# One record of 512 columns for the high weights times high and low activations, in the products that VectorE adds to the residual

## What is computed

```python
# first block
u = causal_dwconv(h @ w_up[l], ffn_conv_w[l], ffn_conv_b[l])
u_gate, u_val = jnp.split(u, 2, axis=-1)
x = x + gate_f * ((jax.nn.silu(u_gate) * u_val) @ w_down[l])
...
# second block, per layer
h = h + hybrid_mixer(rmsnorm(h, norm_mix_g[layer]), ...)       # ends in y @ w_mix_out
h = h + memory_cross_attention(rmsnorm(h, norm_x_g[layer]), ...)   # ends in o @ w_xo
hn = rmsnorm(h, norm_ffn_g[layer])
h = h + swiglu(hn, ffn_w_gate[i], ffn_w_up[i], ffn_w_down[i])   # layer 0
```

## Time and profile before

| | |
|---|---|
| median of 3 runs | 2247.67 us (2243.6 to 2249.77) |
| profiled execution | 2247.01 us, span 2245.3 us |
| TensorE busy | 2183.2 us (97%) |
| VectorE busy | 1701.4 us (76%) |
| ScalarE busy | 1296.6 us (58%) |
| DMA | 563.82 MB, mean 251 GB/s |
| mean granted TensorE clock | 0.99 of 2.4 GHz |

### The profile page before, as it was taken

The page is one execution under the profiler, slowest core; times in us unless marked ns, Lnnn a source line. Parts: engine busy times, 40 slices in busy tenths (PEclk is TensorE's granted clock), DMA queues, the critical chain, the costliest instruction groups (busy, mean ns, idle before and its releaser), DMA issues.

```text
span 2245.3 us, 34129 instructions
## 1 busy us (share of the span) xinstructions
PE 2183.2 (97%) x13631; PEld 1948.4 (87%) x13631; DVE 1701.4 (76%) x1889; ACT 1296.6 (58%) x1289; POOL 76.1 (3%) x159
## 2 busy tenths in 40 slices
PE   7999999999999999999999999999999999999997
PEld 5989988999989899999898888888887888888886
DVE  6768967884785465558654888888888888888887
ACT  3564434763425444443344777777777777777775
POOL 5002200000000000000000000000000000000000
PEclk9999999999999999999999999999999999999999
DMA  9746858655635366555372799999999999999995
GB/s 287 193 127 217 269 175 236 175 173 178 175 116 173 104 170 177 181 155 156 116 239 81 268 365 361 369 329 365 359 369 350 321 370 362 364 345 358 365 365 184
DMA packets 414601, 563.82 MB, mean 251 GB/s; under 512 B 17098, under 2 KB 268212, under 8 KB 414448
## 3 DMA queue, kind: packets, MB, share of 16 engines
q1 hardware_dynamic: 409680, 555.26, 73.5%
q0 software_dynamic: 4768, 6.36, 1.2%
HBM read 559.75 MB, written 1.84 MB: 250 GB/s over the span
## 4 chain that ended last, share of the span: by engine, by line
PE 83%; DVE 8%; ACT 2%; issue 1%; DVEq 0%; ACTq 0%
PE pair L1174 59%; PE misc L1174 13%; PE pair L1234 4%; DVE wlo L1808 2%; DVE opf L1876 2%; PE misc L1717 1%; DVE wlo L2157 1%; PE pair L1685 1%; ACT whi L674 1%; PE misc L1274 1%; PE misc L1253 0%; DVE hl L1827 0%; PE misc L1694 0%; PE misc L1695 0%; PE misc L1365 0%
## 5 line engine op out<-in xcount | busy, mean ns | idle before, releaser
L2157 DVE TENSOR_TENSOR wlo<-raw,whi 128x2048 fp32r<-128x2048 f32 x336 | 764.2, 2290 | 119.6 <-ACT whi L1056 118.9
L1056 ACT CAST whi<-raw 128x2048 fp32r<-128x2048 f32 x336 | 643.1, 1917 | 205.0 <-PE pair L1174 123.5
L1808 DVE TENSOR_TENSOR wlo<-raw,whi 128x2048 fp32r<-128x2048 f32 (+2 forms) x158 | 348.5, 2209 | 157.9 <-ACT whi L674 157.2
L1174 PE MATMUL pair<-hh,whi 128*128 128x256 f32 x1408 | 405.5, 288 | 8.4 <-DVE opl L1827 4.1
L1174 PE MATMUL pair<-hl,whi 128*128 128x256 f32 x1408 | 400.7, 285 | 0.0
L1174 PE MATMUL pair<-hh,wlo 128*128 128x256 f32 x1408 | 400.4, 284 | 0.0
L1174 PE MATMUL pair<-whi,oph 128*128 128x512 f32 x896 | 353.5, 395 | 5.2 <-issue 4.5
L1174 PE MATMUL pair<-wlo,oph 128*128 128x512 f32 x896 | 350.0, 391 | 0.0
L1174 PE MATMUL pair<-whi,opl 128*128 128x512 f32 x896 | 349.7, 390 | 0.0
L674 ACT CAST whi<-raw 128x2048 fp32r<-128x2048 f32 (+2 forms) x158 | 290.1, 1837 | 84.7 <-PE pair L1174 66.8
L1174 PE MATMUL pair<-oph,whi 128*128 128x256 f32 x976 | 279.4, 286 | 5.2 <-issue 3.0
(11 more groups left out here) (464 smaller groups left out, 2788.1 us busy)
## 6 DMA issues: line engine op xcount, KB each, us to landing
raw<-in_moe_w_gate_dram SPq DMA_DIRECT2D x112, 1024.0 KB, 7.1
raw<-in_moe_w_up_dram SPq DMA_DIRECT2D x112, 1024.0 KB, 7.3
raw<-in_moe_w_down_dram SPq DMA_DIRECT2D x112, 1024.0 KB, 7.0
raw<-in_w_in_dram SPq DMA_DIRECT2D x38, 1024.0 KB, 6.1
raw<-in_w_mod_dram SPq DMA_DIRECT2D x24, 1024.0 KB, 5.7
raw<-in_w_up_dram SPq DMA_DIRECT2D x44, 512.0 KB, 5.2
raw<-in_w_xkv_dram SPq DMA_DIRECT2D x16, 1024.0 KB, 5.7
raw<-in_ffn_w_gate_dram SPq DMA_DIRECT2D x22, 512.0 KB, 4.1
```

Source lines behind the costliest of these rows:

```text
L1056: act.copy(whi[:, q, :], raw[:, r, :]).then_inc(sem("hi_ready"), 1)
L1174: ins = pe.matmul(out_, lhs, rhs, start=start and i == 0, stop=stop and i == 2)
L1808: dve.tensor_tensor(wlo[:, i_ % SPLIT, 0:size], raw[:, raw_of(n), 0:size], whi[:, i_ % SPLIT, 0:size].bitcast(F32), ALU.subtract).then_inc ...
L2157: dve.tensor_tensor(wlo[:, q, :], raw[:, r, :], whi[:, q, :].bitcast(F32), ALU.subtract).then_inc(sem("lo_ready"), 1)
```

## The change

High and low activations are laid out as one tensor each: `hx` holds `hh` and `hl`, `opx` holds `oph` and `opl`, so that one operand can reach both parts of a chunk. Five stages stand in `TWO_SUMS`. In these, a triple becomes two matmuls (`both`): the high weights times both parts of the activations, in one record of 512 columns whose operand is two stretches of 256 with a jump between them, into the two halves of a bank; then the low weights times the high activations, 256 columns, into the first half. The bank then holds two sums: the second half has the high weights times the low activations, and VectorE adds it to the residual too, before the first half, each addition waiting for the one before (`link`). `up2` has code for the same form, but is not in the list, and so keeps `three`, as do all other stages.

```diff
+TWO_SUMS = ("down", "mixout0", "mixout1", "xo0", "down2")
...
-        hh = sb("hh", [P, DC, T], F32R)
-        hl = sb("hl", [P, DC, T], F32R)
+        hx = sb("hx", [P, 2, DC, T], F32R)
+        hh, hl = hx[:, 0], hx[:, 1]
...
-        oph = sb("oph", [P, 24, T], F32R)
-        opl = sb("opl", [P, 24, T], F32R)
+        opx = sb("opx", [P, 2, 24, T], F32R)
+        oph, opl = opx[:, 0], opx[:, 1]
...
+            def both(out_, w_hi, w_lo, x, start, stop):
+
+                pe.matmul(out_.rearrange("p (k t) -> p k t", k=2), w_hi, x, start=start, stop=False)
+                return pe.matmul(out_[:, 0:T], w_lo, x[:, 0], start=False, stop=stop)
...
                             col = slice(m * P, (m + 1) * P)
-                            ins = three(pair[:, q, m, 0:T], wh[:, col], wl[:, col], operand(xh, x), operand(xl, x), start, stop)
+                            parts = operand(x_parts, x)
+                            if groups[g][0] in TWO_SUMS:
+                                ins = both(pair[:, q, m, :], wh[:, col], wl[:, col], parts, start, stop)
+                            else:
+                                ins = three(pair[:, q, m, 0:T], wh[:, col], wl[:, col], parts[:, 0], parts[:, 1], start, stop)
...
+            def second(g):
+
+                return pair[:, pair_seq[g] % PAIRS, :, T:2 * T]
+
             def add_modulated(g, j, gate):
                 ps = group(g)
+                if groups[g][0] in TWO_SUMS:
+                    for m in range(2):
+                        t = 2 * j + m
+                        ins = dve.scalar_tensor_tensor(xT[:, t], second(g)[:, m], mod[:, gate + t:gate + t + 1], xT[:, t], ALU.mult, ALU.add)
+                    link(ins)
...
             def add_plain(g, j):
                 ps = group(g)
+                if groups[g][0] in TWO_SUMS:
+                    link(dve.tensor_tensor(xT[:, 2 * j:2 * j + 2, :], second(g), xT[:, 2 * j:2 * j + 2, :], ALU.add))
                 dve.tensor_tensor(xT[:, 2 * j:2 * j + 2, :], ps, xT[:, 2 * j:2 * j + 2, :], ALU.add).then_inc(sem("dve_read"), 1)
...
                     for j, g in enumerate(stage_groups["down2"]):
                         ps = group(g)
-                        link(dve.tensor_tensor(down_n, ps, rt[:].unsqueeze(1).to_broadcast([P, 2, T]), ALU.mult))
+                        by_token = rt[:].unsqueeze(1).to_broadcast([P, 2, T])
+                        link(dve.tensor_tensor(down_n, second(g), by_token, ALU.mult))
+                        link(dve.tensor_tensor(xT[:, 2 * j:2 * j + 2, :], down_n, xT[:, 2 * j:2 * j + 2, :], ALU.add))
+                        link(dve.tensor_tensor(down_n, ps, by_token, ALU.mult))
                         dve.tensor_tensor(xT[:, 2 * j:2 * j + 2, :], down_n, xT[:, 2 * j:2 * j + 2, :], ALU.add)\
                             .then_inc(sem("dve_read"), 1)
```

More of the change, by code:

```diff
@@ L1276, in sums, with into_norm @@
                     ins.then_inc(sem("squares_summed"), 1)
-            def into_norm(stage, name, xh, xl, beside=None, **how):
+            def into_norm(stage, name, x_parts, beside=None, **how):
                 each = how.pop("each_chunk", None)
                 for j, g in enumerate(stage_groups[stage]):
-                    dense_group(g, xh, xl, each_chunk=each if j == 0 else None, **how)
+                    dense_group(g, x_parts, each_chunk=each if j == 0 else None, **how)
                     if j >= 1:
@@ L1475, in _ @@
             for i, g in enumerate(stage_groups["up"]):
-                dense_group(g, hh, hl, each_chunk=h_chunk(1) if i == 0 else None)
+                dense_group(g, hx, each_chunk=h_chunk(1) if i == 0 else None)
                 if i == 0:
@@ L1483, in _ @@
             pe.wait_ge(sem("mem_ready"), DC)
-            into_norm("down", "mix0", oph, opl, beside=stage_groups["xk0"][0], each_chunk=lambda c: (sem("u_lo"), c + 1))
+            into_norm("down", "mix0", opx, beside=stage_groups["xk0"][0], each_chunk=lambda c: (sem("u_lo"), c + 1))
             for l in range(2):
@@ L1491, in _ @@
                     for g in stage_groups[f"{stage}{l}"]:
-                        dense_group(g, hh, hl, each_chunk=h_chunk(k0) if first else None)
+                        dense_group(g, hx, each_chunk=h_chunk(k0) if first else None)
                         first = False
@@ L1609, in _ @@
                 if l == 0:
-                    into_norm("xo0", "ffn0", hh, hl, each_chunk=lambda c: (sem("xo_lo"), c // 2 + 1))
+                    into_norm("xo0", "ffn0", hx, each_chunk=lambda c: (sem("xo_lo"), c // 2 + 1))
                     for i, g in enumerate(stage_groups["up2"]):
-                        dense_group(g, *fin, each_chunk=h_chunk(NORM["ffn0"]) if i == 0 else None)
+                        dense_group(g, fin_at, each_chunk=h_chunk(NORM["ffn0"]) if i == 0 else None)
                         if i == 0:
@@ L1618, in _ @@
                     pe.wait_ge(sem("mem_ready"), 2 * DC)
-                    into_norm("down2", "mix1", lambda c: up2_out(0, c), lambda c: up2_out(1, c), beside=stage_groups["xk1"][0],
+                    into_norm("down2", "mix1", up2_parts, beside=stage_groups["xk1"][0],
                               each_chunk=lambda c: (sem("u2_lo"), c + 1))
@@ L1641, in _ @@
             for j, g in enumerate(stage_groups["xo1"]):
-                dense_group(g, hh, hl, each_chunk=(lambda c: (sem("xo_lo"), 4 + c // 2 + 1)) if j == 0 else None)
+                dense_group(g, hx, each_chunk=(lambda c: (sem("xo_lo"), 4 + c // 2 + 1)) if j == 0 else None)
                 if j >= 1:
@@ L2331, in _ @@
                                 dve.wait_ge(sem("up2_silu"), j - 2)
-                            dve.tensor_tensor(gate_n[:, j % 3], ps[:, 0], rt[:], ALU.mult).then_inc(sem("up2_gate"), 1)
+                            if groups[ups2[j]][0] in TWO_SUMS:
+                                dve.wait_ge(sem("up2_second"), j + 1)
+                                both = up_sum[:, j % 3]
+                                link(dve.tensor_tensor(both, ps, both, ALU.add))
+                            else:
+                                both = ps
+                            dve.tensor_tensor(gate_n[:, j % 3], both[:, 0], rt[:], ALU.mult).then_inc(sem("up2_gate"), 1)
                         if j >= 1:
```

45 lines of the change are left out of this document (26 added, 19 removed).

## The result

| | before | changed |
|---|---|---|
| median of 19 runs | 2248.28 us (2243.6 to 2251.98) | 2254.95 us (2248.34 to 2262.71) |
| ratio, 95% interval | | 1.0029 (1.0019 to 1.0039) |
| profiled execution | 2247.01 us, span 2245.3 | 2249.94 us, span 2248.2 |
| mean granted clock over the runs | 0.989 | 0.987 |

The changed kernel is slower, by 6.7 us in the medians. The forecast was 2248.0 us, with a range to 2252.5; the time lies above it. The profiled execution is the second fastest of the 19, so it shows only 2.9 us of the rise. The rest has to be told from the clock of all runs. The clock given for the kernel before is that of its 105 runs beside the experiments.

What follows compares the result with a forecast made beforehand. TensorE, busy 97% of the span, was taken as the bound. Stage terms -2.0 + 1.5 - 0.8 - 0.9 + 1.5 = -0.7 us, plus 1.5 us for the clock, gave 2248 us; range 2243 to 2252.5 us.

Steps and rivals of the forecast that it cites:

- The loop in `mixout`: VectorE and ScalarE loop lengthens from 6.19 to 6.92 us; TensorE stalls 2.3 us before chunk 6, +1.5 us each layer.
- Rival A: In mixout the loop does not stretch and all record saving is kept: -5.4 us, 2241.6 us; chance 0.10.
- The ends: Added VectorE additions delay the root after the last record: 0.3 us after down, 1.4 us after down2.
- The records: In the five stages, 544 merged triples each save 13.1 ns of fixed record time, 7.1 us in all.
- B: Rival: the record in two stretches costs as two, 239.8 ns; 2253.6 us, or 2255 with a second fall; chance 0.06.
- C: Rival: merging saves only a small fixed part, 1.4 us in all; 2252.5 us; chance 0.04.
- 2.3 us for each of the two long stages: Record saving forecast for down and for down2, 176 triples each at 13.1 ns.
- 0.84 us for `xo0`: Record saving of xo0's 64 triples, expected to be kept in full because chunk 6 just fits, by 0.3 us.
- The full 13 ns a triple: A triple on TensorE goes from 359.7 to 346.6 ns, 13.1 ns less, in all five stages.
- the sum without the clock: Net of down, mixout0, xo0, down2 and mixout1: -2.0 + 1.5 - 0.8 - 0.9 + 1.5 = -0.7 us.
- The clock: TensorE falls to 1.2 GHz behind the one-column records after xq0, expected in both layers: +1.5 us against the trace.
- one fall less to two more: Clock falls allowed for, with the spread of the runs, in the forecast's own range of 2244.5 to 2251 us.

Runs made afterwards that it cites:

- experiment 3: Changed kernel, with ScalarE casting the weights one more slot ahead before it waits for the addition; 2243.46 us, 0.9987; again later 2243.12 us, 0.9981.
- experiment 5: Kernel before, with one more VectorE addition of 128x512 tied before each addition in mixout0 and mixout1, no merged records; 2250.89 us, 1.0013.
- experiment 6: Changed kernel without the second addition in mixout0 and mixout1, merged records kept; 2244.12 us, 0.9989.
- experiment 11: Changed kernel with one spare fp32 product on TensorE ahead of the third group of down and of down2; 2254.77 us (one execution).
- Experiment 7: Changed kernel with 5 spare fp32 products on TensorE ahead of chunk 6 of the first xq group, both layers; 2249.67 us, 1.0010.
- experiment 10: Changed kernel, but the wide record reads 512 adjacent columns, the high parts of two chunks; 2254.52 us, 1.0032.
- experiment 2: Changed kernel with only mixout0 and mixout1 in the list; doubled additions stayed in down2; 2260.83 us, 1.0063.
- experiment 8: Changed kernel with the one-column records split behind the first and second xq group, stall kept; 2253.53 us, 1.0024.

## Why the prediction was wrong

Point by point, by its own steps.

- *The loop in `mixout`*: right, and to the hundredth: 6.92 us forecast and measured; a stall of 2.3 us forecast, 2.4 measured, in both layers; none in `xo0`. Experiments 3, 5 and 6 show it from three sides (loop opened, loop lengthened alone, records alone). Rival A falls.
- *The ends*: +0.32 us forecast and measured after `down`, +1.4 us and +1.40 us after `down2`.
- *The records*: the mechanism is right (a fixed part goes with the record, not with the columns, and a jump in the operand costs nothing), so B and C fall. The term "2.3 us for each of the two long stages" was too large, and so was the 0.84 us for `xo0`. The full 13 ns a triple came in `mixout` and in some groups of `down` and `down2`; in the others 6 ns. Over `down` it was 1.4 us, over `down2` 1.5 us, over `xo0` 0.5 us: 2 us less than forecast in all. By experiment 11 it is not the place in the program that decides; what does stays open. This puts the sum without the clock at +1.2 us instead of -0.7.
- *The clock*: this is the step that failed. "A fall costs 1.5 us ... I expect it in both layers: +1.5 us against this trace" counted the fall behind the one-column records and no other. The stall of 2.4 us brings one of its own, over chunks 6 and 7 (12 records at 1.2 GHz, 1.5 us), and then the fall behind the one-column records comes too: two a layer in the profile. The mean clock of the runs was 0.9894 before and 0.9866 after: half speed over 2.1% and over 2.7% of 2250 us, 12.7 us more. As an estimate that costs half of it, 6 us, where the records are dense. With the 1.2 us above that makes about 7 us, against 6.7 us measured. Experiment 7 gives 5.3 us of it back by filling the stall, and the profiles of all kernels agree on where the falls are. Time at 1.2 GHz around the `xq` stages of both layers (windows 715:750 and 1140:1180, from their PEclk): 3 to 7 us in the seven profiles without a stall and with the one-column records unsplit (two of them of one kernel), 7 us with the stalls of 1.7 us, 14 us in the changed kernel and in experiments 7 and 10, 21 us in experiments 2, 8 and 11, and none in the three kernels without a stall that have the split.
- *What the range took from one trace*: the number of falls is a draw in every execution. Away from `xq`, the profiled execution after had no fall in three places where the one before had one (near 1007, 1236 and 1741 us) and had one in two others (near 182 and 1496 us), and so shows 2.9 us; the runs of the changed kernel spread over 14 us. A range of one fall less to two more around one trace was too narrow on the slow side.

## What to carry to other kernels

Additions of 0.7 us, eight in all, on an engine that is idle a fourth of the time can cost about ten: look whether the starts of that engine's repeated instruction follow the bound engine's pace or a longer period of their own, and which casts or waits in the loop could go ahead. Here one more slot of look-ahead opened it, and only then did the change pay. A short stall of TensorE can cost more than its length (2.4 us did here, 1.7 us did not), above all beside stretches of very narrow records: count what it does to the clock behind it, over all runs and not in one profile, and fill it or move the narrow records apart.

## What was not expected of the hardware

- A stall of 1.69 us before the one-column records left the mean granted clock of the runs at 0.990 (experiment 5), one of 2.38 us took it to 0.987. The first cost no more than its own length, the second about as much again as its own. What lies between was not measured.
- The pace of one and the same sequence of records (512 columns, 256 columns) has settled values, 347 or 353 ns a pair, that hold for a whole group and repeat to a few nanoseconds in every kernel whose groups were measured; spare products ahead of the group can switch them (experiment 11). Triples of 256 columns ran at 120 ns a record in the slopes of 132, 240 and 936 records.
- The split of a stretch of one-column records, 3.6 us into two of 1.8, took 4 us off the kernel before, although its two halves took as long as the whole.
